# A four-engine decoder trunk: projecting the dilated heads job by job inside their own attention

## The reference, cut to what matters

```
y = hn @ w_in          # dq, dk, dv: 3 x 768 columns; then NSA's q, keys, values and gates
dilated heads: 3 groups g of (window, dilation) = (128,1), (512,4), (2048,16), 4 heads each
   logits = q . k[t - offsets] / 8 + T5 bias;  p = softmax;  o_g = p @ v
   o = sum over g of softmax_g(lse_g) * o_g               # merged by softmax denominators
NSA, 4 query heads, one shared key/value head per branch:
   compressed branch (63 block keys, from an MLP over 32-token blocks),
   selected branch, window branch;   o = sigmoid gates x branches
out = concat(o_dil, o_nsa) @ w_out
```

## Time and profile before

| what | us |
|---|---|
| median of 3 runs | 3148.02 (3146.64 to 3150.43) |
| the profiled execution, whole | 3148.97 |
| its span, first to last instruction | 3147.1 |
| PE busy in the span | 2893.8 (92%) |
| PEld / DVE / ACT / POOL busy | 2369.8 / 1163.1 / 858.6 / 924.8 |
| mean granted clock of TensorE | 0.965 |

### The profile page before, as it was taken

One profiled execution on the slowest core, in us unless ns is written; L12 is line 12 of the kernel. 1 busy time (PEld: TensorE's weight loads), 2 busy tenths in 40 slices (PEclk: granted clock), 3 DMA queues, 4 the chain that ended last, 5 costly groups with the idle time before them and its releaser, 6 DMA issues.

```text
span 3147.1 us, 36744 instructions
## 1 busy us (share of the span) xinstructions
PE 2893.8 (92%) x13588; PEld 2369.8 (75%) x13588; DVE 1163.1 (37%) x1849; ACT 858.6 (27%) x1489; POOL 924.8 (29%) x610
## 2 busy tenths in 40 slices
PE   8997888889999999999999975667899999999998
PEld 5786777767888888886788865656668888888867
DVE  3426777314222222225423134467162222222254
ACT  3305666332110000025210024556330000011151
POOL 2330145342333333342233201122413333333332
PEclk9999999999999999999999986889999999999999
DMA  4355422211111111111235267664201111111112
GB/s 154 120 171 158 126 68 61 81 40 34 48 53 47 47 47 47 53 54 54 80 127 210 80 164 141 107 159 113 84 31 47 47 53 47 47 47 47 65 37 74
DMA packets 91069, 257.03 MB, mean 82 GB/s; under 512 B 26211, under 2 KB 29795, under 8 KB 90647
## 3 DMA queue, kind: packets, MB, share of 16 engines
q1 hardware_dynamic: 76008, 199.74, 22.6%
q10 hardware_dynamic: 14944, 55.74, 4.6%
HBM read 207.24 MB, written 52.93 MB: 83 GB/s over the span
## 4 chain that ended last, share of the span: by engine, by line
PE 82%; DVE 8%; DMA 3%; issue 3%; ACT 2%; SPq 1%; POOL 1%; DVEq 0%; ACTq 0%; POOLq 0%
PE ACC L1111 68%; PE ACC L1257 4%; PE OP L1294 3%; PE TR L1271 3%; DMA QK<-y_odds 2%; PE OP L1181 2%; DVE XL L1737 1%; DVE PT L1894 1%; DVE H L1757 1%; SPq L723 1%; DVE T L1754 1%; ACT PT L1531 1%; DVE PB L1877 1%; PE OP L1284 1%; DVE XF L1928 1%
## 5 line engine op out<-in xcount | busy, mean ns | idle before, releaser
L942 POOL CAST WH<-RAW 128x1024 fp32r<-128x1024 f32 x203 | 214.1, 1055 | 1551.9 <-PE ACC L1111 1524.1
L1111 PE MATMUL ACC<-XH,WH 128*128 128x512 f32 x1792 | 574.9, 402 | 47.7 <-DVE XL L1737 26.8
L1111 PE MATMUL ACC<-XL,WH 128*128 128x512 f32 x1792 | 557.9, 393 | 0.0
L1111 PE MATMUL ACC<-XH,WL 128*128 128x512 f32 x1792 | 556.1, 392 | 0.0
L944 POOL TENSOR_TENSOR WL<-RAW,WH 128x1024 fp32r<-128x1024 f32 x203 | 491.0, 2419 | 24.8 <-POOL WH L942 1.5
L1111 PEld LDWEIGHTS ACC<-XH,WH 128*128 128x128 f32 x1792 | 337.6, 189 | 146.8 <-issue 66.4
L1111 PEld LDWEIGHTS ACC<-XL,WH 128*128 128x128 f32 x1792 | 339.8, 190 | 71.9
L1111 PEld LDWEIGHTS ACC<-XH,WL 128*128 128x128 f32 x1792 | 339.5, 189 | 72.1
L1492 ACT ACTIVATE HH<-T 128x1024 fp32r<-128x1024 f32 x64 | 67.9, 1061 | 1149.7 <-DVE T L1779 1149.7
L1786 DVE TENSOR_TENSOR M<-M,ACC 128x1024 f32<-128x1024 f32 x128 | 156.3, 1221 | 482.7 <-PE ACC L1111 480.5
L1111 PE MATMUL ACC<-HH,WH 128*128 128x512 f32 x1024 | 316.6, 390 | 3.3 <-DVE M L1786 3.1
(11 more groups left out here) (200 smaller groups left out, 3284.8 us busy)
## 6 DMA issues: line engine op xcount, KB each, us to landing
RAW<-in_w SPq DMA_DIRECT2D x203, 512.0 KB, 3.4
QK<-y_odds SPq DMA_DIRECT2D x128, 256.0 KB, 6.2
y_odds<-HALVES ACTq DMA_DIRECT2D x16, 1024.0 KB, 5.2
QK<-y_foxs SPq DMA_DIRECT2D x48, 256.0 KB, 5.4
y_foxs<-HALVES ACTq DMA_DIRECT2D x8, 1024.0 KB, 5.0
BIAS<-y_f SPq DMA_DIRECT2D x8, 512.0 KB, 6.9
y_kv<-Q ACTq DMA_DIRECT2D x8, 512.0 KB, 2.6
H<-in_xT ACTq DMA_DIRECT2D x8, 512.0 KB, 7.3
```

Source lines behind the costliest of these rows:

```text
L942: nc.gpsimd.tensor_copy(WH[:, slot], RAW[:, slot]).then_inc(s_whi, 1)
L1111: mm = nc.tensor.matmul(acc[:, h * HALF:(h + 1) * HALF], w(k), x[:, k, h * HALF:(h + 1) * HALF], start=first and k == k0 and w is ws and x ...
```

## The change

The 18 tiles of q, k and v of the dilated heads (kind "dil", one tile for q, k or v of a dilation and a head pair) are no longer split or stored. DVE multiplies such a tile with `R` straight into SBUF: q and k into `QF` (two slots), v into `RV`. The logits of a dilated job are one plain f32 matmul of 64 rows for each task.

Only the three tiles of the first job are projected ahead of attention, beside the six others that the NSA branches need: nine tiles in `in1p`, `in1q` and `in1c`. The other 15 (segment `mix`) are projected during attention: while job n of the dilated ones runs, the q, k and v of job n+1, 8 contraction chunks each, laid out over the 16 steps by `UNIT_STEPS` (three times: two chunks in each of three steps, one in the fourth, and the last one ahead of the logits of the fifth). They share one half of `ACC`, so the first chunk of a tile waits for DVE's evacuation of the tile before; dilated logits have the two banks of the other half. The sixth dilated job (d16 of pair 1) runs with nothing beside it. Order of jobs: all six dilated ones, cmp 0, cmp 1, and then sel and win as before. The queries of both cmp jobs get places of their own in `QK`, and are loaded once the last mixed tile is done; sel 0 can load head e once cmp 0 has made its logits of e. The bias of dilated jobs has its own buffer in two slots. `DU` is doubled; the merge of pair 1 starts 16 steps later, which is again cmp 1. The W1 weights of `compress` (4 MB) are loaded at the start of the projection. The matmuls for the compressed keys move into `in1c`.

The core of the diff:

```diff
+    segs.append(("in1p", 1, [full("odd", 6, 0, "x1"), full("odd", 7, 0, "x1"), full("dil", 0, 0, "x1"),
+                             full("dil", 1, 0, "x1")]))
+    segs.append(("in1q", 1, [full("dil", 2, 0, "x1"), full("odds", 12, 0, "x1"), full("odds", 13, 0, "x1"),
+                             full("oddk", 14, 0, "x1")]))
+    segs.append(("in1c", 1, [full("oddk", 15, 0, "x1")]))
+    segs.append(("mix", 1, [full("dil", c, 0, "x1") for c in range(3, 18)]))
...
-ODD_JOBS = ([(k, 0) for k in DILATED] + [("cmp", 0)] + [(k, 1) for k in DILATED] + [("cmp", 1)]
+ODD_JOBS = ([(k, p) for p in range(2) for k in DILATED] + [("cmp", 0), ("cmp", 1)]
             + [("sel", 0), ("win", 0), ("sel", 1), ("win", 1)])
+UNIT_STEPS = (0, 0, 1, 1, 2, 2, 3, 4)
...
-        depth = 4 if t.small else 2
-        t.acc = t.no % depth
+        depth = 4 if t.kind == "cmp" else 2
+        t.acc = 2 + t.no % 2 if t.kind in DILATED else t.no % depth
...
+            if st.logits and st.logits.kind in DILATED:
+                n, i = divmod(s, 2 * NB)
+                for m in range(3 if n < 5 else 0):
+                    for k in range(DC):
+                        if 5 * m + UNIT_STEPS[k] == i:
+                            (st.early if k == DC - 1 else st.late).append((3 * n + m, k))
+                            if k == DC - 1:
+                                st.ended = 3 * n + m
...
+        # SP, odd layer
+                if name == "odd":
+                    for n in range(6):
+                        if n < 4:
+                            weights("mix", slice(3 * n + 3, 3 * n + 4))
+                        if n:
+                            sums_out(dilated[n - 1])
+                            if dilated[n - 1].kind == "d16":
+                                sums_in(dilated[n - 1])
+                            if n < 5:
+                                dilated_bias(dilated[n + 1])
+                        if n < 4:
+                            weights("mix", slice(3 * n + 4, 3 * n + 6))
+                        if n == 3:
+                            weights_in(dilated[2])
...
+        # POOL
+                for u in mix[0:2] if name == "odd" else ():
+                    split_unit(u)
                 for st in ph.steps:
+                    if st.ended is not None and st.ended + 2 < len(mix):
+                        split_unit(mix[st.ended + 2])
...
+        # PE, logits of a dilated task
+                        q, k = (QF[t.job.slot][rows, m, token(kind, b0):token(kind, b0) + c * (n - 1) + 1:c]
+                                for m, b0, n in ((0, t.i, P), (1, t.blocks[0], w)))
+                        nc.tensor.matmul(score_bank(t), q, k, start=True, stop=True).then_inc(s_qk, 1)
...
+                def project(u, k):
+                    t, slot = u.tiles[0], u.no % 2
+                    if k == 0:
+                        pe.wait_ge(s_split, u.no + 1)
+                        evacuated([t], 0)
+                    mm = three_pass(ACC[:, t.pair], k, k + 1, ...
                 for st in ph.steps:
+                    for no, k in st.early:
+                        project(mix[no], k)
...
+                    for no, k in st.late:
+                        project(mix[no], k)
...
+        # DVE, evacuation of a dilated tile; in attention it stands ahead of the step's scores
+                if t.kind == "dil":
...
+                    dst = RV[:] if m == 2 else QF[j.slot][:, m]
+                    V_.tensor_tensor(dst, ACC[:, t.pair], R[:], ALU.mult).then_inc(s_evD, 1)
```

More of the change, by code:

```diff
@@ L277, in build_attention @@
             j.before = jobs[-1] if jobs else None
+            earlier = lambda ok: next((x for x in reversed(jobs) if ok(x)), None)
+            j.turned = earlier(lambda x: x.kind != "cmp")
+            j.stacked = earlier(lambda x: x.kind not in DILATED and (kind != "sel" or x.kind != "cmp" or x.pair == 0))
+            j.place = int(kind == "cmp" and pair == 1)
+            j.same = earlier(lambda x: x.kind in DILATED and x.slot == j.slot) if kind in DILATED else None
+            j.uses = j.same.uses + 1 if j.same else 1
             jobs.append(j)
             ph.jobs.append(j)
-            n["load"] += {"fox": 1, "mla": 2, "cmp": 0, "sel": 2, "win": 2}.get(kind, 1)
+            n["load"] += {"fox": 1, "mla": 2, "sel": 2, "win": 2}.get(kind, 0)
             j.load, j.head, j.bias, j.raw, j.ops = n["load"], [0, 0], [0, 0], [0, 0], [0, 0]
             for e in range(2):
-                n["bias"][e] += kind not in ("mla", "cmp")
-                n["head"][e] += {"mla": 0, "cmp": 2}.get(kind, 6)
+                n["bias"][e] += kind not in ("mla", "cmp") + DILATED
+                n["head"][e] += 0 if kind in DILATED else {"mla": 0, "cmp": 0}.get(kind, 6)
                 n["raw"] += 3 * (kind == "mla")
@@ L643, in program @@
         seg_end = {n: s.iters[-1][-1].tiles_end for n, s in segs.items()}
+        dilated = [j for j in phases["odd"].jobs if j.kind in DILATED]
+        mix = segs["mix"].iters[0]
+        dil = [t for name in ("in1p", "in1q", "mix") for u in segs[name].iters[0] for t in u.tiles if t.kind == "dil"]
         def prob(t):
@@ L829, in attention @@
                         last_bias = j
-                    if before and before.kind in DILATED:
-                        sums_out(before)
-                        if before.kind == "d16":
-                            weights_in(before)
+                    if j.kind == "cmp" and j.pair == 1:
+                        sums_out(dilated[5])
+                        sums_in(dilated[5])
+                    if j.kind == "sel" and j.pair == 0:
+                        weights_in(dilated[5])
             def store_out(name):
@@ L1246, in logits @@
                     span = lambda x, b0, m: x[:, token(kind, b0):token(kind, b0) + c * (m - 1) + 1:c]
-                    q, ql = (span(QK[:, e, m], t.i, P) for m in range(2))
+                    q, ql = (span(QK[:, e, m], t.i, P) for m in (t.job.place, 1))
                     if kind == "cmp":
@@ L1277, in values @@
                     pe.wait_ge(s_ptD, c.d)
+                    if c.opens and name == "odd" and c.job is dilated[0]:
+                        pe.wait_ge(s_kcd, 1)
                     if c.opens and c.half.prior:
@@ L1545, in attention @@
                 for st in ph.steps:
+                    if name == "odd" and st.logits and st.logits is dilated[0].tasks[8]:
+                        last = tiles[seg_end["in1c"] - 1]
+                        for k in range(2):
+                            act.wait_ge(s_store[k], 16 * last.store[k])
+                        act.wait_ge(s_vst, 32)
                     if st.out:
@@ L1868, in scores @@
                         dve.wait_ge(s_bd, 16 * 7)
+                    elif t.first_of_head and t.kind in DILATED:
+                        dve.wait_ge(s_biasd[t.job.slot], 16 * t.job.uses)
                     elif t.first_of_head:
```

278 lines of the change are left out of this document (167 added, 111 removed).

## The result

| kernel | median us | lowest to highest | runs |
|---|---|---|---|
| before | 3148.68 | 3146.64 to 3150.43 | 4 |
| after | 3113.31 | 3113.01 to 3120.95 | 4 |

The ratio is 0.9889 (0.9873 to 0.9904): the change is faster, by 35 us (1.1%) and not by the 95 forecast, and 3113 lies outside the range. The profiled execution is the longest of the four, 3120.95 us with a span of 3119.1. In it sel 0 makes its first logits at 2029.6 (forecast 1969.9), and the projection behind attention begins at 2199.8, where before it began at 2228.3.

A forecast was written before the change was run, and what follows sets the result against it. Projection was taken as PE-bound, the stretch to sel 0 as load-bound with PE idle 88 us. 1921.1 + 13 + 33.8 + 2 = 1969.9, 94.8 before 2064.7, so 3148.0 becomes 3053 (61%, own range 3043 to 3065); whole range 3034 to 3080.

The forecast's parts named there:

- The logits: Dilated jobs: the new plain f32 matmul of 64 rows costs 0.42 us a wide task, 0.31 a narrow one.
- lower bound: Dilated logits without any cost for height: 0.22 us wide and 0.11 narrow, read from the nearest rows.
- Height: Dilated logits: switching between 64 and full rows adds 0.2 us a task; rival, it hides: 16 us less, 3037, 12%.
- Stride: d4 and d16 tasks: half pace for strided f32 would add 0.11 to 0.22 us each, some 13 us; not taken.
- mixed part: Five dilated jobs with 15 tiles projected among them: 163.2 + 74.8 + 3 = 241.0 us, to 1921.1.
- The sixth job: Last d16 job, before the cmp jobs: 13 us instead of 14.8, its PE work falling to 10.6.
- cmp, sel and win: After the dilated jobs: cmp keeps 33.8 us, plus 2 for POOL; what follows sel 0's start keeps its time.
- The ahead part: Nine tiles projected before attention: 98.0 + 17.2 = 115.1 us, to 1678.7.
- The loads' 69.7 us of waits: Between projection and sel 0, PE waited 42.9 us for `RV` and 26.8 for `QK`; this idle time goes.
- sel 0's stall: PE held by loads before sel 0's first logits: 13.9 us, which goes; rival, it stays: 3067, 10%.
- the stream of weights: Weights for the 15 interleaved tiles have 30 us of lead; rival, each comes late, say 10 us: 3203, 4%.
- The single bank: Half of `ACC` shared by interleaved tiles: 3 us of waits; rival, every tile waits, 24 us: 3074, 12%.

The follow-up runs named there:

- ceiling kernel: After, with dilated tokens written side by side for contiguous operands and logits over all 128 rows (two heads added up): 3060.07 us, ratio 0.9726.
- one-pass kernel: After, with `QF` stored as fp32r, so dilated logits are one 64-row fp32r pass without the low halves: 3074.35 us, ratio 0.9756.
- unmixed kernel: After, with all 15 later tiles projected ahead of the first dilated job and nothing interleaved, logits unchanged: 3150.99 us, ratio 1.0016.

## Why the prediction was wrong

Its sum is 60 us short at sel 0's first logits (2029.6 for 1969.9), and 60 against the medians. By its own steps:

**The logits, the step that failed.** "The new logits are one f32 matmul of 64 rows", with a lower bound of 0.22 and 0.11 us, read off "four plain f32 matmuls of 128 columns" in the earlier trace rows. Those four records are two value matmuls, each recorded twice; so one instruction takes 0.24 for 128 columns, and the bound was half of what the row shows. The count was there to see: one group of four stands for a chunk of two tasks. The ceiling kernel puts the true floor at 0.44 and 0.21. The experiments divide the 33.6 us that the logits' line has over its forecast. With contiguous operands the line is 42.5, which is the ceiling's 26.7 and the forecast's own 0.2 a task for height: the misread floor is 13 of the 33.6. The other 21, from 42.5 to 63.6, are the stride, which the forecast put at nothing.

The Trainium skill, FP8 and Floating Point Precision, section TensorE Precision Notes, has true FP32 as four passes through the array. The trace agrees: 0.44 us for 256 columns at 2.4 GHz is 4.1 cycles a column, shown as two records. The prediction cited this rule and took a misread row over it. By the rule its sum would have been 13 us higher, which is what the floor turned out to lack.

**Height.** It was priced at 0.2 us a task, and on the logits' own line that was right with contiguous operands (42.5 against 26.7) and a little low with strides (63.6 against 43.0, 0.25 a task). Undoing it gave 0.4, since another 12 us went from the projection, value and transpose matmuls beside the logits, to which the forecast gave nothing.

**Stride.** "If a strided f32 operand streams at half pace" was the right question, and "I take neither" the wrong answer: contiguous operands gave 22 us of the mixed part and 28 in all. The 13 us at which the forecast priced it, without taking it, was too low as well, since that stood on the misread floor. The sign of it was in the rows of before: two fp32r records of 256 columns take 0.32 us from start to start in d1 and 0.63 in d4, and the only difference is the stride.

**The sixth job.** 25.3 instead of 13. An estimate: its 16 logits at 0.77 instead of 0.31 make 7.4 us more of PE's work, 18.0 instead of 10.6, and the other 7.3 go with the clock, which fell to 0.50 although PE had no gap. With contiguous or full-height operands it stayed at 1.00 and the job took 12 to 15. What the clock answers to here is not settled: in the one-pass kernel it fell too, from 1.00 to 0.72, and that job took 16.6; in the unmixed one it fell in the first job already, with contiguous operands.

**cmp, sel and win.** The cmp jobs were 0.8 us over their forecast of 35.8. Sel and win took 6.6 more than before, at a granted clock of 0.88 against 0.92. In the profiled executions of the experiments, in which nothing of sel and win was changed, the same stretch took 164.5 to 170.7 at 0.93 to 0.87, so the 6.6 lie within the spread of executions. The profiled one of after is 7.5 longer than the next, and the medians miss the same 60 us that it misses at sel 0's first logits.

**Right.** The ahead part (115.2). The loads' 69.7 us of waits and sel 0's stall are gone. In the mixed part PE never waits on POOL or SP, so the stream of weights keeps up. The single bank costs nothing in after; as a rival it came true only where VectorE's evacuation was made longer, or nothing covered it. So the mechanism of the gain held: between the start of attention and sel 0, PE stood still for 88 us before and for 3.6 after. The new logits, with the neighbours and the clock that go with them, took 60 of the 95 back.

## What to carry to other kernels

Before an instruction is priced from neighbouring rows, divide the number of records by the number of instructions that the code issues: a plain f32 matmul leaves two. A matmul that replaces two in a higher-precision split isn't cheaper for being one; here plain f32 at full height with contiguous operands took 0.43 us for 256 columns against 0.32 for the fp32r pair, and half height or a stride made it dearer. Where work is evacuated from one shared bank, put the instruction that frees the bank first, and whatever completes the tile behind it; that it belongs on the engine with slack only the trace shows here, not the times.

## What the hardware showed that I had not expected

- Height and stride add up, and cost slightly more together. By the median over its tasks a wide f32 logits takes 0.43 us (full, contiguous), 0.63 (half, contiguous), 0.89 (full, stride 4) and 1.20 (half, stride 4): 0.20 and 0.46 apart, 0.77 together.
- The Trainium skill, SBUF — State Buffer, section Door 1: The DMA port swizzle, gives SBUF 16-byte cachelines, says that an access that crosses to a new line pays a penalty, and puts how far one can stride for free at "4 fp32". The rows don't go with the letter of that figure: a step of 4 elements, 16 bytes, already doubles the time at full height (0.43 to 0.89 wide, 0.22 to 0.44 narrow). By the lines themselves each element of such a step is a new one; that this is the cause no run tries. A step of 8 costs about the same as one of 4: 0.45 by the median for a narrow task of the first d16 job at full height.
- The 64-row strided logits take the same time at both clocks. In the sixth job of after, at 0.50, a narrow one still takes 0.77 us, as at 1.00 (0.76), while four value matmuls beside it take 1.02 instead of 0.48. A contiguous 64-row logits does go by the clock: in the first job of the unmixed kernel, at 0.50, a wide one takes 1.15, against 0.63 at 1.00. So it is with the stride that the time stops following the clock; that the reading of the operand is what bounds it was not tried by itself. The DMA engines are not the cause: between 1980 and 1993 they are idle (a share of 0.01) and the tasks take the same 0.77.

```profile
1976.00:1979.50 3.50, 3.50 (x12) 2.50 (x12) 1.31 (x7) 1.17 (x5) 0.00 (x0) 0.50 1.02 233
```
```profile
1976.72 1.23 PE L1376 MATMUL OP<-PF,VF 128*128 128x128 f32 x4
1977.74 0.42 PE L1361 MATMUL TR<-IDENT,PBS 128*128 128x128 f32 x1
1978.09 0.84 PE L1328 MATMUL ACC<-QF 64*128 64x128 f32 x2
1978.86 0.48 PE L1361 MATMUL TR<-IDENT,PBS 128*128 128x128 f32 x1
```

The last fence is of the unmixed kernel, a contiguous wide task at 0.50:

```profile
1893.00 1.22 PE L1323 MATMUL ACC<-QF 64*128 64x256 f32 x2
1894.15 0.69 PE L1356 MATMUL TR<-IDENT,PBS 128*128 128x128 f32 x2
```

- VectorE's evacuation of 128 x 1024 takes 1.23 us when it writes in a row (d1), and 1.93 to 2.00 when it scatters in steps of 1 KB or 512 bytes (d4, d16). A plain copy of 64 rows in SBUF that meets a GpSimd subtraction ends 0.54 to 0.56 us behind it, however early it began, as if it made no progress until then; no copy ran without such a meeting, so its own time isn't measured. GpSimd itself copies the same 64 rows in 1.04.

```profile
L1119 POOL COPY QX<-QF 64x1024 f32<-64x1024 f32 x5 | 5.2, 1040 | 0.3
```
